# Taking the products of the identity with itself out of TensorE's instruction stream, at eleven places of each pair of layers

## What is computed

```python
for l in range(2):      # first block
    h = rmsnorm(x, g_mix[l]); parts = split(h @ w_in[l])
    o_a = mla_attention(...)      # 8 heads, softmax
    o_c = retention(...)          # 4 heads, then a norm and a gate
    o_b = dsa_attention(...)      # 4 heads, softmax over the 128 best keys of each query
    x = x + concat(o_a, o_b, o_c) @ w_out[l]
    x = x + square(relu(rmsnorm(x) @ w_ff1[l])) @ w_ff2[l]
x = rmsnorm(x, g_final)
for l in range(2):      # second block
    parts = split(rmsnorm(h) @ w_in[l])
    o_nsa = native_sparse_attention(...)      # 6 heads: compressed, selected, window
    o_sb = stick_breaking_attention(...)      # 4 heads
    o_gdn = gated_deltanet(...)               # 6 heads, chunks of 64
    h = h + concat(o_gdn, norm(o_nsa), norm(o_sb)) @ w_out[l]
    h = h + conv_ffn(rmsnorm(h)); h = h + gate * rmsnorm(p[l] @ w_ple[l])
return rmsnorm(h, ln_final)
```

## Time and profile before

| | |
|---|---|
| median of 3 runs | 3170.96 us (3170.54 to 3171.04) |
| the profiled execution, its own time | 3171.36 us |
| its span, first to last instruction | 3169.3 us |
| mean granted TensorE clock over the span | 0.994 |
| TensorE busy | 3076.0 us, 97% of the span |
| VectorE, ScalarE, GpSimd busy | 57%, 41%, 13% |

### The profile page before, as it was taken

How to read it: one execution, slowest core, us unless ns; L and a number is a source line. 1 busy time by engine, 2 the same in 40 slices (tenths; PEclk the granted TensorE clock), 3 DMA queues, 4 the chain that set the end, 5 groups by cost and what they waited for, 6 DMA issues and landing times. The chain is left out here.

```text
span 3169.3 us, 48184 instructions
## 1 busy us (share of the span) xinstructions
PE 3076.0 (97%) x19220; PEld 2618.1 (83%) x19220; DVE 1810.4 (57%) x3220; ACT 1288.5 (41%) x2673; POOL 402.4 (13%) x398
## 2 busy tenths in 40 slices
PE   8999999999999999999999999999999999999997
PEld 6878888888878888888888888888888878888886
DVE  4876443435965434357566467474575665574655
ACT  4445432334354423244374343232643643332325
POOL 1031000001031000002213302010003034010010
PEclk9999999999999999999999999999999999999999
DMA  4110222222201322322100122223222000222221
GB/s 176 57 54 28 94 93 98 102 84 89 83 2 54 107 93 94 125 74 100 67 1 2 42 80 100 90 93 117 81 101 80 1 2 22 94 97 95 91 95 63
DMA packets 37293, 239.38 MB, mean 76 GB/s; under 512 B 4432, under 2 KB 5200, under 8 KB 15056
## 3 DMA queue, kind: packets, MB, share of 16 engines
q1 hardware_dynamic: 36080, 233.58, 21.6%
q10 hardware_dynamic: 992, 2.73, 0.3%
HBM read 234.19 MB, written 2.10 MB: 75 GB/s over the span
## 5 line engine op out<-in xcount | busy, mean ns | idle before, releaser
L278 PE MATMUL ps<-b_hl,bff_whl 128*128 128x512 f32 (+1 forms) x840 | 313.6, 373 | 0.0
L279 PE MATMUL ps<-b_hl,bff_whl 128*128 128x512 f32 (+1 forms) x840 | 313.2, 373 | 0.0
L280 PE MATMUL ps<-b_hl,bff_whl 128*128 128x512 f32 (+1 forms) x840 | 313.2, 373 | 0.0
L261 DVE SCALAR_TENSOR_TENSOR bff_whl<-ring,b_cols,bff_whl 128x512 fp32r<-128x512 f32 (+3 forms) x288 | 194.7, 737 | 186.4 <-ACT bff_whl L248 186.1
L248 ACT ACTIVATE bff_whl<-ring,b_cols 128x512 fp32r<-128x512 f32 (+3 forms) x288 | 173.4, 674 | 168.7 <-PE ps L280 168.7
L278 PE MATMUL ps<-a_hl,aff_whl 128*128 128x512 f32 (+1 forms) x648 | 238.9, 369 | 0.0
L279 PE MATMUL ps<-a_hl,aff_whl 128*128 128x512 f32 (+1 forms) x648 | 238.5, 368 | 0.0
L280 PE MATMUL ps<-a_hl,aff_whl 128*128 128x512 f32 (+1 forms) x648 | 238.5, 368 | 0.0
L258 DVE TENSOR_TENSOR aff_whl<-ring,aff_whl 128x512 fp32r<-128x512 f32 x160 | 99.8, 686 | 216.6 <-ACT aff_whl L246 216.5
L278 PE MATMUL ps<-aff_whl,a_hl 128*128 128x512 f32 (+5 forms) x544 | 204.9, 377 | 4.5 <-DVE a_hl L680 2.2
L279 PE MATMUL ps<-aff_whl,a_hl 128*128 128x512 f32 (+5 forms) x544 | 202.3, 372 | 0.0
(11 more groups left out here) (512 smaller groups left out, 7240.7 us busy)
## 6 DMA issues: line engine op xcount, KB each, us to landing
ring<-in_a_w_ff SPq DMA_DIRECT2D x64, 1024.0 KB, 4.7
ring<-in_b_w_up SPq DMA_DIRECT2D x32, 1024.0 KB, 4.8
ring<-in_a_w_in SPq DMA_DIRECT2D x16, 1024.0 KB, 4.8
ring<-in_b_w_down SPq DMA_DIRECT2D x16, 1024.0 KB, 4.8
ring<-in_b_w_in_att SPq DMA_DIRECT2D x12, 1024.0 KB, 4.7
ring<-in_b_w_up SPq DMA_DIRECT2D x16, 768.0 KB, 4.1
ring<-in_b_w_in_conv SPq DMA_DIRECT2D x12, 768.0 KB, 4.2
ring<-in_a_w_out SPq DMA_DIRECT2D x8, 1024.0 KB, 4.9
```

What stands on the lines that cost most here:

```text
L261: self.c.nc.vector.scalar_tensor_tensor(out=self.part(j, 1, k), in0=src[:, k, :], scalar=g[:, row + k:row + k + 1], in1=self.part(j, 0, k) ...
L278: nc.tensor.matmul(bank, sh, mh, start=start, stop=False)
L279: nc.tensor.matmul(bank, sh, ml, start=False, stop=False)
L280: return nc.tensor.matmul(bank, sl, mh, start=False, stop=stop)
```

## The change

All calls of `stay_busy` and the function itself go. Nothing else is edited. That is 40 transposes in each layer of the first block and 74 in each layer of the second, 228 in all.

```diff
@@ -175,11 +175,6 @@
-    def stay_busy(self, pe, bank, n):
-        for _ in range(n):
-            self.nc.tensor.transpose(self.ps[:, bank, 0:P], self.ident, self.ident)
@@ -507,7 +502,6 @@
             if len(jobs) >= 8:
                 wait_kept(len(jobs) - 8)
-            c.stay_busy(pe, len(jobs) % 8, 8)
@@ -2638,7 +2632,6 @@
                     if guest is not None:
                         guest.tensor(pe, i)
-                c.stay_busy(pe, 0, 8)
@@ -3343,7 +3335,6 @@
                     ins.then_inc(outs, 1)
-                c.stay_busy(pe, 0, 32)
@@ -3790,8 +3781,6 @@
-                    if i == 1:
-                        c.stay_busy(pe, 6, 8)
                     u = i - 2
@@ -3815,8 +3804,6 @@
                         if tiles[0] == 0:
-                            if h == SB_H - 1:
-                                c.stay_busy(pe, 0, 10)
                             pe.wait_ge(weights, u + 1)
```

## The result

The changed kernel takes 3180.3 us (median of 8 runs, 3176.6 to 3185.1) against 3170.75 (8 runs of the kernel before, 3168.1 to 3174.6). The ratio is 1.0031, with a 95% interval of 1.0022 to 1.0040: slower by 9.6 us, where 0.8 us less was forecast. The profiled execution took 3179.91 us, its span is 3178.0, 8.7 above the span of before. The intervals of the ratios reach some 3 us to either side.

A forecast was written before the change was run, and what follows sets the result against it. TensorE is busy 97% of the span, but stage ends often wait for other engines: 3.96 us gained against 3.2 us of clock price, so 3170.96 - 0.76 = 3170.2 us, range 3168.2 to 3173.0 (chance 0.72).

The forecast's parts named there:

- The stage ends and the end of stick-breaking: Where TensorE is last, removal starts the next stage earlier: 0.96 us in the first block, 3.00 in the second, 3.96 gained.
- The delta scan's end: Ahead of the output projection, 4.7 us idle makes the clock fall for certain: 1.3 us a layer, 2.6 in two.
- Into stick-breaking: At that stage's start idle time grows from 0.77 to 1.65 us; a fall in one layer of four at 0.66: 0.3.
- All other gaps stay near or below 1.5 us; nothing: Gaps other than the delta scan's end, into retention and into stick-breaking were priced at no clock cost.
- Into retention: Gap grows from 2.09 to 2.97 us; falls go from one layer in two to some three in four: 0.3 us cost.
- the case of 3177.3 or more: Rival, chance 0.04: the clock falls at the delta scan's end and stays low while the dense output projection runs.
- The case of several bounded falls (+4.9): Rival, chance 0.08: two stretches at the delta scan's end, one fall into retention and stick-breaking, in each layer: 3175.8 us.
- The forecast's own range: Whole kernel, small gain against small clock price: 3168.2 to 3173.0 us, chance 0.72.
- ScalarE hides the delay of the third score product: Inside stick-breaking, eight transposes delay that product, but ScalarE is still busy, so removal gains nothing; uncovered, up to 0.9 us per layer.
- The Trainium skill's rule on transpose mode: Transposes don't count as TensorE being busy the same way, making the change all gain; the prediction said the trace disagrees.

The follow-up runs named there:

- the run with the first block alone: Only the products at the ends of the first block's four attention stages taken out of the kernel before, 40 per layer: 3173.57 us against 3170.33, ratio 1.0012.

## Why the prediction was wrong, point by point

- **The stage ends and the end of stick-breaking**: right. 0.13 and 0.20 us for the first transposes and MLA heads, 0.12 ahead of the delta inverse, 1.32 measured for 1.38. The DSA heads show their 0.18 where the clock did not fall (23.83 in place of 24.01 in the second layer of the run with the first block alone). Together 3.9 us of the 3.96 are there.
- **The delta scan's end**: right in mechanism and size, 1.08 and 1.16 us alone, 1.65 and 1.28 in the changed kernel, for a price of 1.3. The clock fell there in all six layers without the 32 and came back within the transposes.
- **Into stick-breaking**, the step that failed most: "No single gap is over 2 us; a fall here in one layer out of four, at 0.66: 0.3". The fall came in both layers of both profiled executions without the filler behind the sparse heads and the one behind the second score (before: in none). It cost 4.71 us a layer alone, and 4.7 and 3.2 us in the changed kernel (46.48 and 44.91 against 43.08 - 1.32), not 0.66. I took the price of a fall from stages with one stretch and carried it to a stage where the clock stayed down for 10 to 14 us, once for 41. That stage is a ring: TensorE, VectorE and ScalarE wait for each other. In most of the low stretches TensorE's records fill the time (3.40 of 3.40 us) and VectorE and ScalarE stand idle for much of it, so there TensorE paces the ring, where ScalarE had at full clock at the stage's start. Why the clock stays low although TensorE shows as busy, when in the projection (299.10 to 302.50 us, 3.40 of 3.40 too) it came back after one stretch, is not shown. No run changed the ring.
- **"All other gaps stay near or below 1.5 us; nothing"**: this failed too, for some 3.8 us in the first block alone (1 to 7 by its interval). The clock fell behind gaps of 1.38 us (DSA heads, 0.47 net of the 0.18 won) and of 1.00 us (projection, 1.17). I had set a size of gap from a single fall; the row of that fall shows only that 2.09 us can be enough. And the kernel before had already shown that less can be. The fall whose price of 1.53 I used, into the delta scan from 1766.90 us on, came at the end of 0.77 us of idle time (its timeline, then its stretch):

```profile
1765.58 0.68 PE L3165 MATMUL ps<-b_work,b_work 64*64 64x64 f32 x8 [0.34 <-ACT b_work L3198]
1767.03 1.79 PE L3311 MATMUL ps<-b_work,b_kbe 128*64 128x128 f32 x10 [0.77 <-PEq L168]
...
1766.90:1770.30 3.40, 3.27 (x26) 3.30 (x28) 0.00 (x0) 0.38 (x1) 0.74 (x1) 0.50 0.03 7
```

The one in the sparse heads at 1565.5 came 2.2 us behind the end of a wait of 1.04 us.

- **Into retention**: 2.96 us of idle time, as worked out, and a fall in one layer of the changed kernel's two, but it cost 1.7 us and not 0.66, and "one layer in two" for 2.09 us came from two layers; over nine kernels it is 3 of 18.
- **The rivals**: 3180.3 lies in the case of 3177.3 or more, which had 0.04. That case, a clock that does not come back, named the right mechanism at the wrong place: I looked for it in the dense projection, where the clock came back, not in the stage with the ring of waits. The case of several bounded falls (+4.9) named some of the right places, at too low a price. The forecast's own range was also added up a little too narrow: gains of 3.5 to 4.3 and prices of 1.3 to 6.0 give 3168.0 to 3173.5, not 3168.2 to 3173.0.
- **ScalarE hides the delay of the third score product**: right. In the run without those eight, with the clock still up, its activation for the third unit starts 3.36 us into the stage, where it was 3.39. What they were worth was the clock.
- **The Trainium skill's rule on transpose mode**: my reading of the trace against it held for these transposes. They hold the clock (at the delta scan's end in 16 of 16 layers with the 32, and in none of 6 with nothing there), and ordinary products of the same width do no better.

## What to carry to other kernels

Products that nobody reads can be worth more than their time: before taking them out, ask at each place which engine is last there, and what TensorE does in the next 10 us if its clock falls. Where engines wait for each other in a ring, a fall at its start can last for a large part of the stage, so fill the gap ahead of it first; where TensorE is last (here the eighteen at the end of stick-breaking), the filler costs its time, so take it out if the trace then shows no new fall. Price a fall by a stage of the same kind, not by the nearest one that happens to show a fall, and take its chance from the same place in several executions, not from the length of the idle time alone.

## What was not expected of the hardware

- Fillers that keep TensorE as busy in the profile can differ in what they do for the clock: ordinary products of 64 columns, 7.3 us slower over the kernel, all in stick-breaking as far as the profile shows; of 128 columns, the same as transposes (0.9994 to 1.0011).
- The low clock is not always one stretch of 3.4 us: 13.7 us and 10.2 us in the changed kernel, 41 us once.
- One kernel's executions spread with their mean granted clock: 3169.9 us at 0.993 to 3188.0 us at 0.987 without the filler behind the sparse heads. What decides in an execution which gaps meet a fall was not tried.
- Idle time of 0.8 us (into the delta scan, a fall in 9 of 24 layers) was followed by low clock no less often than 2.1 us at another place (into retention, 3 of 18).
